# Hybrid decoder layer, last stage: norm scaling, block sums, product order and residual additions placed differently

## The reference

```python
def merge_and_ffn(x, y_ssm, y_attn, g_ssm, g_attn, w_ssm_out, w_attn_out, w_o, norm2_g, w_up, w_down):
    mix = jax.nn.sigmoid(g_ssm) * (y_ssm @ w_ssm_out) + jax.nn.sigmoid(g_attn) * (y_attn @ w_attn_out)
    x = x + mix @ w_o
    h = rms_norm(x, norm2_g)
    return x + jnp.square(jax.nn.relu(h @ w_up)) @ w_down
```

## Time and profile before

| | us |
|---|---|
| median of 3 runs (1895.53 to 1899.97) | 1899.54 |
| profiled execution | 1902.16 |
| its span, first to last instruction | 1899.9 |
| PE busy in the span | 1686.4 |
| DVE, ACT, POOL busy in the span | 1103.4, 745.5, 732.7 |

### The profile page before, as it was taken

How to read it: one execution, slowest core, us unless ns; L and a number is a source line. 1 busy time by engine, 2 the same in 40 slices (tenths; PEclk the granted TensorE clock), 3 DMA queues, 4 the chain that set the end, 5 groups by cost and what they waited for, 6 DMA issues and landing times. The chain is left out here.

```text
span 1899.9 us, 31479 instructions
## 1 busy us (share of the span) xinstructions
PE 1686.4 (89%) x12434; PEld 1553.8 (82%) x12448; DVE 1103.4 (58%) x1845; ACT 745.5 (39%) x1358; POOL 732.7 (39%) x474
## 2 busy tenths in 40 slices
PE   3989879978999988787899987779999959999997
PEld 2969639978999955554699987779999949999997
DVE  4850657899865537553242139565455456776775
ACT  5232445655433435443222334334444332333332
POOL 8101104875110000000544345434444356677770
PEclk6989979998999999999899998889999979999999
DMA  5122161212852114005552422343453555444422
GB/s 150 50 74 78 37 76 49 87 57 85 152 140 102 38 55 135 1 1 179 168 162 81 136 74 82 102 147 126 142 168 127 198 205 175 154 135 148 137 81 92
DMA packets 162692, 208.28 MB, mean 110 GB/s; under 512 B 20946, under 2 KB 106898, under 8 KB 162514
## 3 DMA queue, kind: packets, MB, share of 16 engines
q1 hardware_dynamic: 162066, 205.58, 35.7%
q0 software_dynamic: 480, 0.69, 0.2%
HBM read 147.45 MB, written 58.78 MB: 109 GB/s over the span
## 5 line engine op out<-in xcount | busy, mean ns | idle before, releaser
L139 PE MATMUL psum<-b_hi,ua_hi 128*128 128x264 f32 x896 | 263.4, 294 | 35.0 <-DVE view_at L3211 16.3
L139 PE MATMUL psum<-db_hi,da_hi 128*128 128x264 f32 x896 | 257.9, 288 | 25.4 <-DVE view_at L3251 19.5
L141 PE MATMUL psum<-b_hi,ua_lo 128*128 128x264 f32 x896 | 261.2, 292 | 0.0
L140 PE MATMUL psum<-b_lo,ua_hi 128*128 128x264 f32 x896 | 261.0, 291 | 0.0
L141 PE MATMUL psum<-db_hi,da_lo 128*128 128x264 f32 x896 | 258.2, 288 | 0.0
L140 PE MATMUL psum<-db_lo,da_hi 128*128 128x264 f32 x896 | 258.2, 288 | 0.0
L3065 POOL TENSOR_TENSOR ua_lo<-view_at,ua_hi 128x512 fp32r<-128x512 f32 x112 | 152.3, 1365 | 179.7 <-ACT ua_hi L2874 179.7
L139 PE MATMUL psum<-h_hi,w_hi 128*128 128x352 f32 x600 | 197.1, 328 | 21.1 <-POOL w_lo L211 19.0
L139 PEld LDWEIGHTS psum<-b_hi,ua_hi 128*128 128x128 f32 x896 | 176.0, 196 | 36.7 <-issue 31.4
L3266 DVE TENSOR_TENSOR view_at<-psum,view_at 128x528 f32<-128x528 f32 x220 | 152.8, 703 | 91.4 <-PE psum L141 91.2
L211 POOL TENSOR_TENSOR w_lo<-view_at,w_hi 128x2048 fp32r<-128x2048 f32 (+1 forms) x19 | 85.9, 4522 | 305.4 <-ACT w_hi L205 305.3
(11 more groups left out here) (403 smaller groups left out, 4039.1 us busy)
## 6 DMA issues: line engine op xcount, KB each, us to landing
hid_dram<-view_at SPq DMA_DIRECT2D x112, 264.0 KB, 2.2
view_at<-hid_dram SPq DMA_DIRECT2D x56, 528.0 KB, 4.0
view_at<-w_in SPq DMA_DIRECT2D x18, 1024.0 KB, 5.5
view_at<-w_up SPq DMA_DIRECT2D x16, 1024.0 KB, 5.9
view_at<-w_down SPq DMA_DIRECT2D x32, 512.0 KB, 6.5
gate_dram<-view_at SPq DMA_DIRECT2D x48, 176.0 KB, 2.1
view_at<-gate_dram SPq DMA_DIRECT2D x16, 528.0 KB, 4.5
view_at<-cache_k SPq DMA_DIRECT2D x32, 256.0 KB, 3.3
```

The lines of the kernel that those rows point to most:

```text
L139: nc.tensor.matmul(out, lhs[0], rhs[0], start=start, stop=False, skip_group_check=more)
L140: nc.tensor.matmul(out, lhs[0], rhs[1], start=False, stop=False, skip_group_check=more)
L141: return nc.tensor.matmul(out, lhs[1], rhs[0], start=False, stop=stop, skip_group_check=more)
```

## The change

It leaves the arithmetic of the layer in place and moves work.

- Norm: `total(0)`, `total(1)`, `mean`, `root` and `scale` of the first two quarters are placed earlier and piece by piece between the output units; `scale` takes a range of channels. B21's low part moves from POOL to DVE.
- Block sums: T1 and T2 are made in two halves of 264 tokens a block row (`sums_b`), the first before the last quarter is scaled. T3's sum and low part move from POOL to DVE; the low parts of T4 (as before) and of B22 (before on DVE) are POOL's. All high and low parts of B and T that were four instructions of 528 columns are one of 2112.
- Products in order 6 7 5 in every chunk of the up phase. u3 is made after product 7 and c22 after product 5 (`sum_22`).
- x1 is no longer loaded into the result blocks: it comes block by block through one buffer, and 16 DVE additions (`add_x1`) are placed between products of steps 1 to 4 of the down phase. `load_raw_b(0)`, `(1)` are issued at chunk 6, `(2)` in chunk 15.
- End: `add_u2` for one block goes to POOL, for the others between the drains; `turn_back` waits for parts and not for all; DVE takes two of the last output pieces.

```diff
-    def h2(r, s, k):
-
-        return xT[:, KH * r + k, TF * s:TF * (s + 1)]
+    def h2(r, s):
+
+        return xT[:, KH * r:KH * (r + 1), TF * s:TF * (s + 1)]
...
-        UJ += [(c_, p_) for p_ in ((6, 5, 7, 4, 3) if c_ < NE else (1, 6, 5, 7, 2, 4, 3))]
+        UJ += [(c_, p_) for p_ in ((6, 7, 5, 4, 3) if c_ < NE else (1, 6, 7, 5, 2, 4, 3))]
...
+    x1b = view(8536, 4, TF)
+    X1_AT = ((0, 2, 3, 4), (0, 1, 2, 3), (0, 1, 2, 4), (0, 1, 2, 3))
+    Y_DVE = (16, 18)
...
             def load_x1(j):
                 _, e, s = BLOCKS[j]
-                sp.dma_start(BLOCKS[j][0], x1_dram[:, 4 * e:4 * e + 4, TF * s:TF * (s + 1)]).then_inc(x1_in[j], 16)
+                for q in range(4):
+                    sp.wait_ge(x1_st[q], 16 * KD)
+                if j:
+                    sp.wait_ge(x1_added, 4 * j)
+                else:
+                    sp.wait_ge(up_mm, U_END)
+                sp.dma_start(x1b, x1_dram[:, 4 * e:4 * e + 4, TF * s:TF * (s + 1)]).then_inc(x1_in, 16)
...
+                if c == NE + 2:
+                    sp.wait_ge(u2_done, NE)
+                    load_raw_b(0)
+                    load_raw_b(1)
                 if c == LASTC:
-                    sp.wait_ge(up_mm, at_u(c, 1) + 1)
-                    load_x1(0)
+                    sp.wait_ge(su_done, 4 * c)
+                    sp.wait_ge(ua_lo, at_u(c - 1, 4) + 1)
+                    load_raw_b(2)
                     sp.wait_ge(up_mm, at_u(c, 6) + 1)
                     load_raw_d(0)
-                    load_raw_b(0)
-                    load_raw_b(1)
...
             sp.wait_ge(up_mm, U_END)
+            sp.wait_ge(da_hi, 2)
+            sp.wait_ge(sd_done, 1)
             load_raw_d(1)
-            for j in range(7):
-                sp.wait_ge(h_st[j], 16 * (NCH - (NE if j == B11 else 0)))
-            for j in (2, 1, 3):
-                load_x1(j)
             for n in range(3, ND):
                 sp.wait_ge(db_lo, n - 2)
                 load_raw_b(n)
                 d, i = divmod(n, 7)
+                if i == 3 and 1 <= d <= 4:
+                    load_x1(d - 1)
...
+            low_b(T4, h2(1, 0))
+            low_u(10)
+            low_b(B22, h2(1, 1))
+            for n in range(11, NU):
                 low_u(n)
...
+            for mt in range(4):
+                pool.wait_ge(drained, 4 * (ND - 5) + mt + 1)
+                tt(CA[Z][:, mt, :], CA[Z][:, mt, :], U2a[:, mt, :], ALU.add).then_inc(z_added, 1)
...
+            def sums_b(u):
+                cols = halves[u]
+                b11, b12, b22 = h2(0, 0)[:, :, cols], h2(0, 1)[:, :, cols], h2(1, 1)[:, :, cols]
+                v.tensor_tensor(b11, b12, b11, ALU.subtract).then_inc(t_sum[0], 1)
+                dve.wait_ge(t_sum[0], u + 1)
+                v.tensor_tensor(t2raw[:, :, cols], b22, b11, ALU.subtract).then_inc(t_sum[1], 1)
...
+            def add_x1(n):
+
+                d, i = divmod(n, 7)
+                if not 1 <= d <= 4 or i not in X1_AT[d - 1]:
+                    return
+                mt = X1_AT[d - 1].index(i)
+                x = BLOCKS[d - 1][0][:, mt, :]
+                dve.wait_ge(x1_in, 16 * d)
+                dve.wait_ge(drained, 4 * n)
+                v.tensor_tensor(x, x, x1b[:, mt, :], ALU.add).then_inc(x1_added, 1)
...
                 if p == 7:
                     sum_z(c)
                     if c + 1 < NCH:
+                        sums_u(c + 1, 3)
+                if p == 5:
+                    sum_22(c)
+                    if c + 1 < NCH:
                         sums_u(c + 1, 4)
-                    else:
-                        low_d(0)
                 if p == 2 and c == LASTC:
+                    low_d(0)
                     low_d(1)
```

More of the change, by code:

```diff
@@ L2506, in hybrid_kernel @@
         raw_b_in = [sem(f"s9_raw_b{j}") for j in range(3)]
-        x1_in = [sem(f"s9_x1_in{j}") for j in range(4)]
+        x1_in = sem("s9_x1_in")
+        x1_added = sem("s9_x1_added")
+        z_added = sem("s9_z_added")
         sd_done = sem("s9_sd")
@@ L2590, in _ @@
             store_e(1)
-            for k in range(2):
-                sp.wait_ge(b_lo[T1], k + 1)
-                sp.wait_ge(b_lo[T3], k + 1)
+            sp.wait_ge(b_lo[T1], 1)
+            sp.wait_ge(b_lo[T3], 1)
             load_u(1)
@@ L2654, in _ @@
                 cols = slice(EH * e, EH * (e + 1))
-                sp.wait_ge(y_done, n + 1)
+                if n in Y_DVE:
+                    sp.wait_ge(y_dve, Y_DVE.index(n) + 1)
+                else:
+                    sp.wait_ge(y_done, n + 1 - sum(1 for m in Y_DVE if m < n))
                 if wp:
@@ L2959, in _ @@
                     residual(RESID[i])
+                square(2 * i)
+                if i == 12:
+                    root(0)
                 if i == 13:
-                    root(0)
-                if i == 14:
                     root(1)
-                    for z in range(2):
-                        act.wait_ge(scaled_q, 2)
-                    for k in range(KH):
-                        high_b(B11, k, h2(0, 0, k))
-                square(2 * i)
+                if i == 15:
+                    root(2)
                 square(2 * i + 1)
@@ L2978, in _ @@
                     high_u(2)
+                if i == 13:
+                    act.wait_ge(scaled_q, 2)
+                    high_b(B11, h2(0, 0))
                 if i == 14:
-                    for k in range(KH):
-                        high_b(B21, k, h2(1, 0, k))
+                    high_b(B21, h2(1, 0))
                     high_u(1)
                     high_u(3)
-                    root(2)
             high_u(4)
@@ L3104, in _ @@
                 if i == 14:
-                    for k in range(KH):
-                        low_b(B21, k, h2(1, 0, k))
                     low_u(1)
@@ new lines, in take_y @@
+            def take_y(n):
+                b, i = divmod(n, 5)
+                dve.wait_ge(yT_done, n + 1)
+                dve.wait_ge(y_st[n % 8], 16 * stored(n, n % 8))
+                v.tensor_copy(yout[0:CUTS[i][1], n % 8, :], psum[0:CUTS[i][1], i, :]).then_inc(y_dve, 1)
+            for n in range(len(OJ)):
+                if n == 25:
+                    scale(0, range(0, 4))
+                if n == 26:
+                    scale(0, range(4, KD))
+                    mean(1)
+                if n == 27:
+                    scale(1, range(0, 4))
@@ L3276, in _ @@
                 if n == 28:
-                    scale(0)
+                    scale(1, range(4, KD))
+                if n == 29:
+                    low_b(B11, h2(0, 0))
                 if n == 30:
-                    scale(1)
+                    low_b(B21, h2(1, 0))
+                if n == 31:
+                    mean(2)
                 add(n)
-            for k in range(KH):
-                low_b(B11, k, h2(0, 0, k))
-            mean(2)
+                if n == 23:
+                    mean(0)
@@ L3302, in _ @@
+            v.tensor_tensor(h2(0, 1), h2(1, 1), h2(0, 1), ALU.subtract).then_inc(t_sum[2], 1)
+            sums_u(0, 3)
+            dve.wait_ge(b_lo[B21], 1)
+            dve.wait_ge(b_lo[T2], 1)
+            v.tensor_tensor(h2(1, 0), h2(1, 0), t2raw, ALU.subtract).then_inc(t_sum[3], 1)
+            low_b(T3, h2(0, 1))
+            low_b(T1, h2(0, 0))
             sums_u(0, 4)
-            for k in range(KH):
-                low_b(B22, k, h2(1, 1, k))
             for n in range(len(EJ), NU):
```

188 lines of the change are left out of this document (85 added, 103 removed).

## The result

| | before | after |
|---|---|---|
| median, runs in turn on the same chip (4 each), us | 1899.76 | 1867.53 |
| lowest and highest, us | 1895.53, 1902.62 | 1864.65, 1869.61 |
| profiled execution, its span, us | 1902.16, 1899.9 | 1869.61, 1867.8 |

The ratio is 0.9831 with an interval of 0.9807 to 0.9855: 32.2 us less. The spans of the two profiled executions differ by 32.1, so their traces can be set against each other.

What follows compares the result with a forecast made beforehand. PE bounds most of the up and down phases; losses stand in the other four windows, with DVE's list holding the norm. Terms 13 + 5 + 14 + 6 = 38 off 1902.2 give 1864.2, as a median 1862; range 1846 to 1879.

Steps and rivals of the forecast that it cites:

- the x1 additions: Down phase: 16 DVE additions priced at 0, since DVE has 1.6 us free a product and late drains cost PE nothing.
- Term A: Norm and block sums: less DVE and POOL work ahead of the first u3, released near 1187 instead of 1200.3; 13 us.
- The prices by extension: Norm operations of 2112 columns, extrapolated from shorter ones: 2.3 us on DVE, 4.7 on POOL.
- The lock: DVE operations with two SBUF inputs and POOL ones run one after the other; the norm gain is then 13 us.
- DVE busy without a break before it: Norm, a sign: DVE works without a gap until PE's wait for the first u3, near 1187.
- no lock: Rival at the norm: DVE and POOL run freely, gain 19 us, total 1856; chance 0.12.
- POOL as the bound: Rival at the norm: POOL's 4.7 us low parts delay weight parts, gain 7 us, total 1868; chance 0.13.
- Term B: Up phase, chunks 1 to 3: order 6 7 5 saves 1.7 us each, 5 in all; u3 waits of 2 to 4 remain.
- the order removes the waits: Rival for chunks 1 to 3: u3 waits and their clock loss go, 25 us in place of 5, total 1842; chance 0.11.
- Term C: Turn to the down phase: early operand loads and less data ahead of the fourth hidden operand restart PE earlier; 14 us.
- The rival for the down phase: x1 additions exceed DVE's free time, drains come late and the clock drops: 50 us lost, total 1912; chance 0.04.
- Term D: End: additions on POOL and between drains remove PE's 4.2 us wait, plus clock and copies; 6 us.

Runs made afterwards that it cites:

- t3_low_pool: The changed kernel with T3's low part back on POOL, its sum still on DVE; 1873.18 us, ratio 0.9867 against the kernel before.
- order_only: The kernel before with only the product order 6 7 5, the split of sum_z and the third S sum's place; 1890.45 us, ratio 0.9966.
- sums_late: The changed kernel with the hidden layer's T sums moved behind u3 and c22 in chunks 1 to 3; 1858.05 us, ratio 0.9804 against before.
- x1_direct: The changed kernel with x1 loaded straight into the result blocks and no later additions, early operand loads kept; 1869.84 us, ratio 0.9842 against before.
- no_adds: The changed kernel without its 16 x1 additions on DVE, the x1 loads kept; 1857.65 us, ratio 0.977 against the kernel before.
- raw_b_first: The changed kernel with w_down's step issued behind the next step's first hidden operand, all additions kept; 1860.27 us, ratio 0.9786 against before.
- end_blocks: The changed kernel with the end's 12 shared-block additions back on DVE in blocks of four and eight; 1868.62 us, ratio 0.9825 against before.

## Why the prediction was right, and where it was not

The median, 1867.5, is 5.5 above the 1862 forecast and inside its own range. The four terms came out within 1.1 us each; the x1 additions, priced at nothing, did not. That the miss is 5.5 and not more is in part luck, for the 9.4 us that the additions cost meet 2.7 that no term accounts for.

- **Term A**, forecast 13, measured 13.6. The first u3 comes at 1183.94; 1187 was said, 2.7 of the difference is earlier start. The prices by extension held: 2.36 for 2112 columns on DVE (2.3 said), on POOL 4.73 in t3_low_pool and 5.17 with waits (4.7 said). The lock carried over as assumed: with POOL's operation out of the way the pair of low parts fell from 10.22 to 5.70. One sign failed, "DVE busy without a break before it": DVE idles 4.33 us for w_up ahead of the first u3, and that load waits for the low parts of T3 and T1. The sum had no such term, so that it came out near is in part luck. If the order is worth the 3.0 us of order_only here too, what A named is worth some 10.6 and was about 2 too large; which of its pieces was not tried. The rival "no lock" is out; POOL as the bound is near (t3_low_pool comes close to it, and PE waits 2.3 us for ua_lo in the changed kernel).
- **Term B**, 5, measured 6.1. Three waits were left as said, here 2.50, 2.56 and 4.08, each 1.5 to 1.7 us shorter than before (1.7 said). sums_late bears out the reasons given, the T sums ahead of u3 and behind them the wait for w_up; order_only rules out that the order removes the waits.
- **Term C**, 14 (its own working gave 14.8), measured 13.8. A wait of 8.11 and one of 5.31 stood where 7 to 9 and about 5 were said. x1_direct shows that the x1 loads ahead of the fourth operand were 7.8 of the 13.8: with them back, the wait is 13.08. The other 6.0 must lie with the early loads of the first three operands and the 5.2 us wait that is gone; that was not tried. That operand landed 21.0 us after the end of the up phase, where near 20 was said, though not by the steps given: w_down was issued 10.4 after that end (11.5 said), and the operand landed 10.65 behind that issue (8.6 said by its share of the bytes, so the bytes are not the whole of such a wait).
- **The x1 additions**, priced at 0, cost the 9.4 us lost in the down phase; without them (no_adds) it is as short as before. This is the step that failed: "I price them at 0", resting on "with 1.6 free" a product on DVE. The sentence weighed DVE's busy share, and there DVE did have time: it idles 1.4 to 4.9 us at the seams, although the 16 additions take 1.49 us each on the mean and the low parts beside them 2.28, where they take 1.80 in no_adds. What it left out is who waits on the other side of the lock. Each addition also holds POOL, POOL's last sum is what releases w_down's next step, and the next hidden operand is queued behind it. In the trace of before that ring went at PE's own step, 40.9 us, and left DVE 0.03 us at one seam; with the additions PE's waits stand 43.1 to 43.6 apart. raw_b_first shows the coupling, since it keeps every addition and gets 8.9 back. The rival for the down phase had the right place but the wrong mechanism and size: late drains by DVE's own load, 50 us. The waits were once a step and not once an addition.
- **Term D**, 6, measured 5.3: the wait of 4.20 is down to 0.27, and the clock of the last window is 1.00 where it was 0.94. end_blocks shows that the placing on POOL and between drains is worth 1.7 of it; how the rest is shared was not tried.
- 2.7 us come from before 1107. 3.1 stand already at the addition before (1106.54 and 1103.44), where the code is unchanged; the first moved mean then costs 0.4. It is scatter: order_only has the code of before up to the third total and starts it at 1127.39, where before has 1133.15. It covers a part of the loss.

## What to carry to other kernels

Before work is added to an engine with idle time, follow who shares a lock or a port with it, and whether the other one stands in a ring of release, DMA issue, load and conversion; a ring that takes as long as the PE step shows next to no wait (0.26 us of DVE at most here) and has little reserve. In a single DMA queue, a small operand that is needed soon belongs ahead of a large one that may only be issued when a buffer comes free. A part of a change that wins at one place and gives it back at another is best found by undoing it as a whole, as x1_direct did.

## What was not expected of the hardware

DVE and POOL took turns on whole instructions: a DVE pair worth 4.7 us took 10.22, and POOL's instruction of 512 columns 3.40. A long instruction is so a high price for short ones on the other engine, 2.1 us for this one.

The stretches at a granted clock of 0.50 (1.2 GHz) followed idle times of PE, but not always the same ones. The code between the first and fourth u3, the same in each, took 59.0 us in one trace (granted clock 0.88) and 55.1 in another (0.97). In the down phase of the changed kernel a wait of 1.73 us was followed by 3.4 us at the lower clock, while the three before it, 1.57 to 1.68 us long, were followed by none.
